# A routed SwiGLU layer: the experts taken in order of their token count, three of them as plain float32 matmuls with 64 token rows on two column halves of the array

## The reference

```python
logits = (xf @ router_w).astype(jnp.float32)
top_logits, top_idx = lax.top_k(logits, TOP_K)          # TOP_K = 2, N_EXPERTS = 8
gates = jax.nn.softmax(top_logits, axis=-1)
...
def swiglu(h, w_gate, w_up, w_down):                    # per expert: 1024 -> 3584 -> 1024
    return (jax.nn.silu(h @ w_gate) * (h @ w_up)) @ w_down
...
ys = swiglu(xs, w_gate[e], w_up[e], w_down[e]) * slot_gate
out = zeros.at[slot_tok].add(ys)
```

## Time and profile before

| | |
|---|---|
| median of 3 runs | 1483.52 us (1482.71 to 1485.45) |
| the profiled execution, whole | 1485.55 us |
| its span, in which the trace's instructions lie | 1483.8 us |
| mean granted PE clock | 0.989 of full speed |
| period from one expert to the next | 122.8 us |
| the experts with the store, share of the span | about 68% |

### The profile page before, as it was taken

The page is one execution under the profiler, slowest core; times in us unless marked ns, Lnnn a source line. Parts: engine busy times, 40 slices in busy tenths (PEclk is TensorE's granted clock), DMA queues, the critical chain, the costliest instruction groups (busy, mean ns, idle before and its releaser), DMA issues.

```text
span 1483.8 us, 17200 instructions
## 1 busy us (share of the span) xinstructions
PE 1438.4 (97%) x7146; PEld 1203.8 (81%) x7146; DVE 1150.1 (78%) x1043; ACT 983.2 (66%) x1075; POOL 0.2 (0%) x4
## 2 busy tenths in 40 slices
PE   7999999999999899999999999999999999999997
PEld 6777999977776688888888888888888888888885
DVE  4666555546763888888898898888889889888885
ACT  5575444435772777777777777777777777777773
POOL 0000000000000000000000000000000000000000
PEclk9999999999998999999999999999999999999998
DMA  9904453474111599999999999999999999999970
GB/s 365 353 1 170 157 185 114 150 265 165 63 44 71 208 367 368 346 358 377 345 352 372 363 346 370 366 344 359 375 344 350 378 353 356 365 373 344 359 284 30
DMA packets 126692, 417.45 MB, mean 281 GB/s; under 512 B 3345, under 2 KB 8081, under 8 KB 126481
## 3 DMA queue, kind: packets, MB, share of 16 engines
q1 hardware_dynamic: 126608, 416.29, 75.5%
HBM read 415.23 MB, written 1.05 MB: 281 GB/s over the span
## 4 chain that ended last, share of the span: by engine, by line
PE 92%; DVE 3%; ACT 3%; issue 1%; DMA 0%; SPq 0%; DVEq 0%; ACTq 0%
PE ps L463 27%; PE ps L464 27%; PE ps L465 27%; PE ps L794 2%; PE ps L445 1%; PE ps L456 1%; DVE scratch L1312 1%; ACT xn L873 1%; PE ps L591 1%; ACT scratch L950 1%; PE ps L736 1%; PE ps L737 1%; PE ps L718 0%; PE ps L720 0%; PE ps L596 0%
## 5 line engine op out<-in xcount | busy, mean ns | idle before, releaser
L1538 DVE TENSOR_TENSOR ring_lo<-ring,e_hi 128x2048 fp32r<-128x2048 f32 x336 | 765.5, 2290 | 112.9 <-ACT e_hi L1097 111.1
L1097 ACT ACTIVATE e_hi<-ring 128x2048 fp32r<-128x2048 f32 x336 | 643.3, 1921 | 224.1 <-PE ps L465 224.1
L463 PE MATMUL ps<-e_hi,xgT_hi 128*128 128x512 f32 x896 | 352.7, 394 | 5.1 <-DVE xgT_lo L1544 5.1
L465 PE MATMUL ps<-e_hi,xgT_lo 128*128 128x512 f32 x896 | 350.0, 391 | 0.0
L464 PE MATMUL ps<-ring_lo,xgT_hi 128*128 128x512 f32 x896 | 349.9, 390 | 0.0
L463 PEld LDWEIGHTS ps<-e_hi,xgT_hi 128*128 128x128 f32 x896 | 168.9, 188 | 39.6 <-DVE xgT_lo L1544 5.3
L465 PEld LDWEIGHTS ps<-e_hi,xgT_lo 128*128 128x128 f32 x896 | 168.7, 188 | 35.5
L464 PEld LDWEIGHTS ps<-ring_lo,xgT_hi 128*128 128x128 f32 x896 | 168.8, 188 | 34.3
L463 PE MATMUL ps<-e_hi,hidT_hi 128*128 128x512 f32 x448 | 175.8, 392 | 0.0
L465 PE MATMUL ps<-e_hi,hidT_lo 128*128 128x512 f32 x448 | 174.6, 390 | 0.0
L464 PE MATMUL ps<-ring_lo,hidT_hi 128*128 128x512 f32 x448 | 174.4, 389 | 0.0
(11 more groups left out here) (239 smaller groups left out, 1538.7 us busy)
## 6 DMA issues: line engine op xcount, KB each, us to landing
ring<-moe_g SPq DMA_DIRECT2D x56, 2048.0 KB, 8.0
ring<-moe_u SPq DMA_DIRECT2D x56, 2048.0 KB, 7.8
ring<-moe_d SPq DMA_DIRECT2D x56, 2048.0 KB, 8.1
ring<-w_in SPq DMA_DIRECT2D x6, 2048.0 KB, 10.8
ring<-dense_g SPq DMA_DIRECT2D x5, 2048.0 KB, 7.8
ring<-dense_u SPq DMA_DIRECT2D x5, 2048.0 KB, 7.9
ring<-dense_d SPq DMA_DIRECT2D x5, 2048.0 KB, 8.7
ring<-w_out SPq DMA_DIRECT2D x4, 2048.0 KB, 14.3
```

The source lines that it names most:

```text
L463: pe.matmul(out, hi_l, hi_r, start=start, stop=False, skip_group_check=True)
L465: return pe.matmul(out, lo_l, hi_r, start=False, stop=stop, skip_group_check=True)
L1097: nc.scalar.activation(hi_slot(g, s, q), slot_of(no)[:, r * E_PIECE:(r + 1) * E_PIECE], ACT.Copy).then_inc(act_done, act_p.step((g, s, "le ...
L1538: nc.vector.tensor_tensor(slot_lo(no)[:, part], slot_of(no)[:, part], hi_slot(g, s, q).bitcast(F32), ALU.subtract).then_inc(dve_done, dve_ ...
```

## The change

Three things, all in the expert stage.

1. `sort` (DVE, new, 22 small instructions) orders the experts by token count. Expert 0 always comes first. The other seven follow so that the places 1, 3 and 6 in the loop (`SMALL_AT`) hold the three with the fewest tokens; SP reads the expert's number from the sorted list (`order`) with a register load at the first unit of each expert and issues transfers with an address from that register.
2. The experts at places 1, 3 and 6 are run by `small_expert`: capacity 64 (`HALF`), and each product as one plain float32 matmul, straight from the ring's slot, with no split by ACT and DVE. The stationary operand has 64 columns, and two matmuls stand side by side: one writes the accumulation partitions 0 to 63 (the left half of the array's columns) with one half of the weight columns, the other partitions 64 to 127 with the other half. A unit is 8 matmuls of 512 columns (or 16 of 256) where it was 24 of 512.
3. The second pass over the experts is now taken if any expert has over 128 tokens or any of the three at places 1, 3 and 6 over 64. The three with the fewest of experts 1 to 7 have 64, 59 and 53. The flag `over_i` is computed inside `sort`, and PE and ACT read it before place 1 instead of before place 0.

```diff
+HALF = GROUP // 2
+N_FULL = 5
+SMALL_AT = (1, 3, 6)
+CAPACITY = [GROUP] * N_FULL + [HALF] * (NE - N_FULL)
+KEY_STEP, KEY_FIRST = 8.0, 8192.0
+S_SCATTER_AFTER = (0, 2)
+S_HID_T_AFTER = {S_LAST["u", c] + 1: c for c in range(NGU)}
+S_PICK_T_AFTER = S_LAST["d", 1] + 1
+S_GATHER_AFTER = S_FIRST["d", NCH - 3]
...
@@ sync, expert_units
+                        if is_small(g, before_s):
+                            sp.wait_ge(pe_done, at((g, before_s, "unit", before_m)))
...
+                    rank = s if g else RANK_AT[s]
+                    if rank == 0:
+                        e = slice(0, 1)
+                    elif m == 0:
+                        sp.wait_ge(dve_done, at("order"))
+                        e = bass.ds(sp.value_load(order[0:1, rank:rank + 1], min_val=0, max_val=NE - 1), 1)
...
@@ tensor, experts
+                def small_unit(s, n):
+                    kind, c, h = MOE_UNITS[n]
+                    w = slot_of(unit_no(g, s, n))
+                    pe.wait_ge(*loaded(unit_no(g, s, n)))
...
+                    if kind == "d":
+                        for j in range(CH // P):
...
+                            for b in range(2):
+                                ins = pe.matmul(ps[b * HALF:(b + 1) * HALF, 4, :], hidT_s[c // 2 % 2][:, tokens],
+                                                w[:, j * D + b * CH:j * D + (b + 1) * CH], start=c == 0 and j == 0,
+                                                stop=c == NCH - 1 and j == CH // P - 1, skip_group_check=True)
+                    else:
+                        cols = GU_COLS[c]
+                        for i in range(UNIT // cols):
+                            k = h * (UNIT // cols) + i
+                            for b in range(2):
+                                part = slice(i * cols + b * cols // 2, i * cols + (b + 1) * cols // 2)
+                                ins = pe.matmul(ps[b * HALF:(b + 1) * HALF, 0 if kind == "g" else 2, 0:cols // 2],
+                                                xgT_s[:, k, :], w[:, part], start=k == 0, stop=k == KD - 1,
+                                                skip_group_check=True)
+                    ins.then_inc(pe_done, pe_p.step((g, s, "unit", n)))
...
+                def small_expert(s):
+                    for n in range(M_UNITS):
+                        small_unit(s, n)
+                        if n in S_SCATTER_AFTER:
+                            scatter_before(S_SCATTER_AFTER.index(n), s, None)
+                        if n in S_HID_T_AFTER:
+                            small_hidden_T(s, S_HID_T_AFTER[n])
...
@@ scalar, experts
+                def small_expert(s):
+                    for b in range(2):
+                        act.wait_ge(pe_done, at((g, s, "gathered", b)))
+                        for k in range(4 * b, 4 * b + 4):
+                            nc.scalar.activation(xgT_s[:, k, :], ps[:, 6 + b, k % 4 * P:k % 4 * P + HALF], ACT.Copy,
+                                                 scale=G("ffn_g", DEPTH - 1)[:, k:k + 1]).then_inc(act_done, act_p.step((g, s, "xgT")))
+                    y_out_before(s, None)
+                    for c in range(NGU):
...
+                        nc.scalar.activation(sig_s[:, 0:w], ps[:, 0, 0:w], ACT.Silu).then_inc(act_done, act_p.step((g, s, "silu", c)))
...
+                    rows_out(s + 1)
```

More of the change, by code:

```diff
@@ L157 @@
 PICKS_AFTER = E_LAST["u", 2]
+HALF = GROUP // 2
+N_FULL = 5
+SMALL_AT = (1, 3, 6)
+RANK_AT = []
+for _s in range(NE):
+    RANK_AT.append(N_FULL + SMALL_AT.index(_s) if _s in SMALL_AT else _s - sum(n < _s for n in SMALL_AT))
+FULL_AT = [_s for _s in range(NE) if _s not in SMALL_AT]
+CAPACITY = [GROUP] * N_FULL + [HALF] * (NE - N_FULL)
+KEY_STEP, KEY_FIRST = 8.0, 8192.0
+S_FIRST, S_LAST = {}, {}
+for _n, (_kind, _c, _h) in enumerate(MOE_UNITS):
+    S_FIRST.setdefault((_kind, _c), _n)
+    S_LAST[_kind, _c] = _n
+S_SCATTER_AFTER = (0, 2)
+S_HID_T_AFTER = {S_LAST["u", c] + 1: c for c in range(NGU)}
+S_PICK_T_AFTER = S_LAST["d", 1] + 1
+S_GATHER_AFTER = S_FIRST["d", NCH - 3]
 class Progress:
@@ L344, in hi_slot, with is_small @@
         def hi_slot(g, s, q):
-            return e_hi[:, (q if g else s * N_E + q) % E_SPLIT, :]
+            return e_hi[:, (q if g else FULL_AT.index(s) * N_E + q) % E_SPLIT, :]
+        def is_small(g, s):
+            return g == 0 and s in SMALL_AT
         def before(g, s, it, *what):
@@ new lines, in sort @@
+                dve.wait_ge(dve_done, own())
+                for a in range(2 * TT):
+                    nc.vector.tensor_tensor(moved[:, a * NE:(a + 1) * NE, :], is_at,
+                                            by_expert[:, a:a + 1, :].broadcast_to([P, NE, NE]), ALU.mult).then_inc(dve_done, dve_p.step())
+                dve.wait_ge(dve_done, own())
+                nc.vector.tensor_reduce(by_rank[:, :, 0:NE], moved.rearrange("p (a n) e -> p a n e", a=2 * TT), AX.X,
+                                        ALU.add).then_inc(dve_done, dve_p.step())
@@ new lines, in sort @@
+                nc.vector.memset(by_rank[:, :, NE:NE + 1], 0.0).then_inc(dve_done, dve_p.step())
+                nc.vector.memset(rank_over[:, :, NE:NE + 1], -1.0).then_inc(dve_done, dve_p.step())
+                dve.wait_ge(dve_done, own())
+                for r0, r1 in ((0, N_FULL), (N_FULL, NE)):
+                    nc.vector.tensor_scalar(rank_over[:, :, r0:r1], by_rank[:, 0:TT, r0:r1], -float(CAPACITY[r0]), None,
+                                            ALU.add).then_inc(dve_done, dve_p.step())
+                    nc.vector.memset(limits[:, r0:r1], CAPACITY[r0] * KEY_STEP + KEY_STEP - 1).then_inc(dve_done, dve_p.step())
```

238 lines of the change are left out of this document (189 added, 49 removed).

## The result

The changed kernel takes **1415.9 us** (median of 4 runs, 1414.4 to 1417.2) against 1484.5 us of the kernel before on the same chip: a ratio of 0.954, 95% interval 0.952 to 0.955. The forecast was 1417 us. The profiled execution has a span of 1415.4 us, 68.4 us shorter than the 1483.8 before.

What follows compares the result with a forecast made beforehand. PE was taken as the bound (97% busy), with transfers only 0.3 to 0.5 us a unit behind. The 1483.8 us span less 66.3 gives 1419.2; the median, 2.0 us below the profiled execution, gives 1417 us, range 1397 to 1462.

Steps and rivals of the forecast that it cites:

- The halves overlap: Small experts: paired plain matmuls run side by side, 3.4 us a unit; rival of no overlap 6.9, 1571 us, chance 14%.
- the return waits for `xgT_lo`: Small to full expert: first unit's landing, lead, `xgT_hi`, subtraction, `xgT_lo` take 6.35 us after landing; PE idle 8.4 us.
- The sort is covered: Before the first expert: 22 small DVE instructions, 4.4 us, lie within DVE's 5.05 us wait; cost 0, up to 1 us.
- the 2.0 us that it was given: Each of three returns to a full expert: matmuls lose 2.0 us to a lowered clock after PE's idle gap.
- The second pass didn't run: Rival, expert loop: one token over capacity 64 reruns all eight experts, 982 us slower, near 2400; chance 2%.
- the two rows named for the matmul's 0.227 us: Full experts: starts at 612.78 and 613.01 cited for 0.227 us a matmul, 24 of them making 5.45 us a unit.
- s: Expert weight transfers: DMA engines' time for one unit under full load, taken as 5.45 us (385 GB/s).
- the way to 1399 us: Expert transfers: at 404 GB/s, 5.19 us a unit, the places gain 28.5, 27.6 and 28.5 us, giving 1399.
- its formula for place 1: First small expert plus return: 8.0 + 14s + s + 6.35 + 2.0 = 98.1 us instead of 122.8, 24.7 less.
- a stock of 4.1 units: Ring before place 3: only 4.1 units stocked after one full expert, so that place takes 105.9 us, 16.9 less.
- the 66.3 forecast: Total saving in us at places 1, 3 and 6: 24.7, 16.9 and 24.7.
- The rival by which the transfers have no margin: Expert transfers: more load brings no more bytes, 5.87 us a unit, 1467 us, barely 1% faster; chance 7%.

## Why the prediction came out right, and where it didn't

**The steps that held.** The halves overlap: 34 records in 7.46 us. The earlier trace rows had let one expect it only from row halves. A small expert is PE work of 82 us (79 forecast) within 92.8 us that the transfers set, which the run with half of the matmuls shows. The second half of a small expert waits for transfers, the return waits for `xgT_lo`, and PE is idle 7.6 us there (8.4 forecast), with a chain of 6.36 us (6.35). The granted clock fell at each return. The sort is covered: its last instruction starts at 484.42, and DVE then still waits 1.75 us for the first lead. (The first expert's first matmul, at 490.74 instead of 490.14, is no test of it, since that start differs by 3 us between runs of one kernel.) The clock's fall costs the 2.0 us that it was given: the extra matmuls take off 1.9, 2.2 and 2.1 us at the three returns. The second pass didn't run. One reading was loose: the two rows named for the matmul's 0.227 us lie 0.23 apart, and a longer run of them gives it (twelve in 2.72 us from 615.50).

**The transfers were faster than I took them for.** This is the term that was mis-sized. s, 5.45 us a unit, was read from the earlier trace rows, 375 to 389 GB/s. In the changed kernel the rate is 409 GB/s, 5.12 us a unit (the two units of each expert with chunks of 512 columns aside, which come at about 385). The earlier trace rows mix two lesser cases. The stretches among the experts are such that a transfer lands 8 to 10 us after its issue, so that one or two are in flight; in the small experts it lands after 15 to 24 us, with three to five in the queue. The stretch 20:60 has a queue as long (20 us from issue to landing), but its weights come in packets of 2 KB (15.46 MB in 7670) where the experts' come in packets of 4 KB (9.83 MB in 2477 from 684 to 708 us of the changed kernel, at 410 GB/s), and so do the 385 GB/s of the chunks of 512 columns. Queue and packet size weren't varied by themselves. The kernel before had a short stretch at the higher rate too, which the mean over 20 us hid:

```profile
685.00:690.00 5.00, 5.00 (x24) 4.14 (x23) 4.95 (x5) 4.26 (x3) 0.00 (x0) 1.00 1.04 404
```

The prediction had named the higher rate as the way to 1399 us. With the measured values its formula for place 1 gives 8.0 + 14 x 5.15 + 5.15 + 6.4 + 1.9 = 93.6 us for the small expert with its clock loss, and 92.8 + 1.9 = 94.7 were measured. And since s is smaller, the ring was full again before place 3: 92.97 us there, like at the other two, where I had 105.9 for a stock of 4.1 units. The page's 24th slice, 363 GB/s around the start of place 3, is the full ring. With the 2.0 us that I had for the clock a place would be 92.9 + 2.0 = 94.9 us, 27.9 less than before, 83.7 in three: 17.4 us more than the 66.3 forecast. The rival by which the transfers have no margin is out: the Trainium skill's limit of about 358 GB/s ("DMA: Bandwidth & Descriptors", Specifications) is passed by 50 GB/s. The Trainium skill ("HBM Reference", Specifications (TRN2)) has about 425 GB/s for a core that streams alone, and this kernel uses one core; the 409 measured agrees with that better.

**What cancelled it.** A full expert was costed at 122.8 us as before, and that term was too small in two ways. All of them are 2.4 us slower, 12 us in five, by the place of their stationary operands. Nothing in the rows of before could have told it, but the new arrays ahead of them were in the diff and should have been a rival. And each of the three behind a small expert takes 1.0 us more with the clock at full, 3 us in all, 2 of them for the small expert's scatters, which the sum put at nothing. So 83.7 - 12 - 3 = 69 against the 66.3 forecast. The result lies that near to the forecast because an error of 17 us in one term met two of 12 and 3 us of the opposite sign, not because each term was right. That is luck.

## What to carry to other kernels

Where a faster stage runs into the transfers, read their rate where the queue is as long and the packets are as large as they will be, and keep both ends: the 0.3 us by which a 2 MB unit was faster were worth 17 us here (6 for each 0.1; the prediction's 11 is too much on this side, where the ring fills up). Whenever a change adds or resizes an array in front of matmul operands, compare the operands' addresses as well as the instructions, and when a matmul's period has moved by some 2% try another place before another theory. At each hand-over from a stage bound by transfers to one with a chain of several engines, do on the chain what doesn't need the transfer while it is under way, and keep PE busy with matmuls nobody reads; expect the gain only where the transfers aren't the bound from one hand-over to the next.

## What the runs showed of the hardware that I had not expected

- With several 2 MB transfers queued, one core drew 402 to 409 GB/s from HBM over more than 100 us (packets of 4 KB; with packets of 2 KB and as long a queue 387); where PE was the bound and freed one slot at a time it was 347 to 372.
- The period of a fp32r matmul of 128 x 512 changes with where its stationary operand lies in SBUF: 0.227 us on average at three addresses, 0.231 to 0.233 at three others, some only 32 bytes from a fast one. In the kernel before, 32 bytes cost 22 us of 1484.
- In the small experts with half of the matmuls the granted clock averaged 0.84 with PE busy 60% of the time, and it made no difference to the time, since PE wasn't awaited.
- A return with 7.6 us of idle PE cost 1.9 to 2.2 us by the clock, about as much as the gap of 5.1 us before the first expert (2.0 worked out from the earlier trace rows, 1.5 given back by the extra matmuls); with matmuls that nobody reads in it the granted clock stayed at 1.00.
